# A two-layer decoder trunk on one core: the moving columns of every split product run from the last to the first

## What is computed

```
zxbcdt = rms(x) @ in_proj                  # 2048 x 10304
h = x + rms(gated_scan(zxbcdt) @ out_proj) # 4096 x 2048
h = h + rms(relu(rms(h) @ w1)**2 @ w2)     # 2048 x 8192, 8192 x 2048
k, v = rms(h) @ w_k, rms(h) @ w_v          # 2048 x 2048 each
h = h + rms(diff_attn(rms(h) @ w_q, k, v) @ o_proj)
h = h + rms(relu(rms(h) @ w1)**2 @ w2)
```

## Time and profile before

| what | value |
|---|---|
| median of three runs | 2656.3 us |
| span of the profiled execution, first to last instruction | 2654.2 us |
| granted TensorE clock, mean over the span | 0.988 of full |
| TensorE streams (PE) busy | 2578.9 us, 97% |
| weight loads (PEld) busy | 2338.9 us, 88% |
| VectorE (DVE) busy | 1805.5 us, 68% |
| ScalarE (ACT) busy | 1203.1 us, 45% |
| HBM read | 470.70 MB, 179 GB/s over the span |

### The profile page before, as it was taken

The page is one execution under the profiler, slowest core; times in us unless marked ns, Lnnn a source line. Parts: engine busy times, 40 slices in busy tenths (PEclk is TensorE's granted clock), DMA queues, the critical chain, the costliest instruction groups (busy, mean ns, idle before and its releaser), DMA issues.

```text
span 2654.2 us, 44813 instructions
## 1 busy us (share of the span) xinstructions
PE 2578.9 (97%) x16616; PEld 2338.9 (88%) x16616; DVE 1805.5 (68%) x2617; ACT 1203.1 (45%) x1589; POOL 138.4 (5%) x261
## 2 busy tenths in 40 slices
PE   6999999999999999999999899999899999999997
PEld 6889988998889898989898888988689999999996
DVE  3777777776876656565656867767876666666666
ACT  3555445544554434343434644444453434343433
POOL 2220222012100000000000000000000000000000
PEclk8999999999999999999999999999999999999999
DMA  8665566556446666566666555555356665666664
GB/s 182 199 189 176 172 192 196 166 181 190 160 141 193 190 190 190 190 190 189 190 189 191 175 167 166 158 175 167 120 169 196 185 194 186 193 186 194 187 193 135
DMA packets 267175, 477.17 MB, mean 180 GB/s; under 512 B 16577, under 2 KB 50210, under 8 KB 265298
## 3 DMA queue, kind: packets, MB, share of 16 engines
q1 hardware_dynamic: 263296, 457.76, 55.7%
q0 software_dynamic: 3296, 18.12, 2.8%
q10 hardware_dynamic: 498, 0.18, 0.0%
HBM read 470.70 MB, written 5.31 MB: 179 GB/s over the span
## 4 chain that ended last, share of the span: by engine, by line
PE 92%; DVE 4%; ACT 2%; issue 1%; DMA 1%; POOL 0%; ACTq 0%; DVEq 0%; POOLq 0%; SPq 0%
PE ps L1241 29%; PE ps L1242 29%; PE ps L1243 29%; PE ps L1387 1%; ACT whl L562 1%; DVE whl L820 1%; ACT junk L565 1%; PE ps L1406 0%; DVE h L929 0%; DVE xhl L890 0%; DMA par_rows<-a_conv_b 0%; PE ps L1466 0%; DVE stat L842 0%; PE ps L1380 0%; PE ps L1390 0%
## 5 line engine op out<-in xcount | busy, mean ns | idle before, releaser
L820 DVE TENSOR_TENSOR whl<-raw,whl 128x1024 fp32r<-128x1024 f32 x865 | 1069.8, 1237 | 771.3 <-ACT whl L562 761.9
L562 ACT ACTIVATE whl<-raw 128x1024 fp32r<-128x1024 f32 x865 | 916.2, 1059 | 1280.6 <-PE ps L1243 1253.9
L1241 PE MATMUL ps<-xhl,whl 128*128 128x256 f32 x3072 | 866.0, 282 | 6.3 <-DVE xhl L890 6.3
L1242 PE MATMUL ps<-xhl,whl 128*128 128x256 f32 x3072 | 859.2, 280 | 0.0
L1243 PE MATMUL ps<-xhl,whl 128*128 128x256 f32 x3072 | 858.7, 280 | 0.0
L1241 PEld LDWEIGHTS ps<-xhl,whl 128*128 128x128 f32 x3072 | 580.1, 189 | 11.4 <-DVE xhl L890 7.7
L1242 PEld LDWEIGHTS ps<-xhl,whl 128*128 128x128 f32 x3072 | 580.2, 189 | 2.9 <-issue 1.7
L1243 PEld LDWEIGHTS ps<-xhl,whl 128*128 128x128 f32 x3072 | 580.0, 189 | 0.0
L1241 PE MATMUL ps<-whl,bhl 128*128 128x512 f32 x1408 | 552.0, 392 | 4.7 <-DVE bhl L951 3.6
L1242 PE MATMUL ps<-whl,bhl 128*128 128x512 f32 x1408 | 550.5, 391 | 0.0
L1243 PE MATMUL ps<-whl,bhl 128*128 128x512 f32 x1408 | 549.9, 391 | 0.0
(11 more groups left out here) (194 smaller groups left out, 1877.6 us busy)
## 6 DMA issues: line engine op xcount, KB each, us to landing
raw<-mlp_w SPq DMA_DIRECT2D x512, 512.0 KB, 4.1
raw<-a_in_proj SPq DMA_DIRECT2D x161, 512.0 KB, 4.5
raw<-a_out_proj SPq DMA_DIRECT2D x64, 512.0 KB, 4.5
raw<-b_w_q SPq DMA_DIRECT2D x32, 512.0 KB, 3.7
raw<-w_k SPq DMA_DIRECT2D x32, 512.0 KB, 3.7
raw<-w_v SPq DMA_DIRECT2D x32, 512.0 KB, 3.7
raw<-b_out_proj SPq DMA_DIRECT2D x32, 512.0 KB, 3.7
cumb<-cum_scratch POOLq DMA_DIRECT2D x8, 1024.0 KB, 7.7
```

The source lines that it names most:

```text
L562: sc.activation(whi[:, s.split, :], raw[:, s.raw, :], ACT.Copy).then_inc(hi_ready, 1)
L820: ve.tensor_tensor(out=wlo[:, s.split, :], in0=raw[:, s.raw, :], in1=whi[:, s.split, :].bitcast(F32), op=ALU.subtract).then_inc(lo_ready, 1)
L1241: te.matmul(outs, lh, rh, start=start, stop=False, skip_group_check=True)
L1242: te.matmul(outs, lh, rl, start=False, stop=False, skip_group_check=True)
```

## The change

The helper `three` turns the moving operand and the output around: both are passed with a step of -1 along the columns. Column n of the moving operand still goes to column n of PSUM, so the values in PSUM are the same; the last column is read, multiplied and written first. The stationary operand, the flags, the order of the products, the waits and the number of instructions are as before.

```diff
             def three(outs, lhs, rhs, start, stop):

-                (lh, ll), (rh, rl) = lhs, rhs
+                (lh, ll), (rh, rl) = lhs, [t[:, ::-1] for t in rhs]
+                outs = outs[:, ::-1]
                 te.matmul(outs, lh, rh, start=start, stop=False, skip_group_check=True)
                 te.matmul(outs, lh, rl, start=False, stop=False, skip_group_check=True)
                 return te.matmul(outs, ll, rh, start=False, stop=stop, skip_group_check=True)
```

## The result

The changed kernel takes 2692.29 us (median of 4 runs, 2690.71 to 2694.12) against 2655.78 us for the kernel before (4 runs, 2653.08 to 2656.63). The ratio is 1.0137, with a 95% interval of 1.0125 to 1.0149: 36.5 us slower. The forecast was no change, 2656 us. The time lies in the stated range, where the rival "the remainder grows" had put 2687 us, but the likeliest case was the wrong one.

A forecast was written before the change was run, and what follows sets the result against it. TensorE was taken to bound the kernel, its products summing to 2403 us of a 2654.2 us span. Column price and remainder each added 0; with 2.1 us from span to run median, the forecast was 2656 us, range 2628 to 2740 us.

The forecast's parts named there:

- the remainder grows: Rival on TensorE: descending stream falls in step with the next stationary operand's load; 31 us more, 2687 us; chance 0.28.
- the likeliest case: Whole kernel: nothing changes, 2656 us, alone from 2650 to 2662 us; chance 0.37, the ineffective form included.
- What bounds the kernel: TensorE, streaming 97% of the span; time follows product distances one to one; loads, ScalarE and VectorE are hidden.
- The terms of the sum: TensorE's products: counts times distances, 1075 + 92 + 958 + 179 + 88 + 11 = 2403 us, 91% of the span.
- the five kinds: TensorE products: 256 columns moving `xhl` or `khl`; 512 columns against stationary `bhl`, `xhl` or `khl`; distances 116.7 to 233 ns.
- 190 us of remainders: Part of the 2403 us of TensorE products left beside 2212 us of columns at one per cycle.
- The price of a column: Moving read and PSUM write on TensorE: taken as unchanged, 0 us; upper bound 2379 us more.
- the rival at 4868 to 5035 us: TensorE: descending read or PSUM write takes two cycles a column; chance 0.18 for this or worse.
- The remainder: TensorE distance beyond one cycle a column, set by placement: taken as unchanged, bounds 90 us more to 28 us less.
- by symmetry: Moving stream's start: reversed, each kind keeps as many words in its first line, so the remainder changes by nought.
- The bound of 6.7 ns for wide products: 512-column `bhl` products: at worst each gains 6.7 ns, the gap between the two wide kinds; 28 us for 4224.
- The chances: Whole kernel: nothing changes 0.37, remainder grows 0.28, remainder shrinks 0.17, two cycles a column or worse 0.18.

The follow-up runs named there:

- run 3: Kernel before with the change made only for the products of 512 columns: 2685.75 us, ratio 1.0112.
- run 2: Kernel before with only the PSUM output written from last column to first, moving operand read ascending: 2656.44 us, ratio 1.0001.
- run 6: Kernel before, moving operand read in ascending blocks of 16 words, the words inside each from last to first: 3005.61 us, ratio 1.1315.
- runs 12 and 15: Kernel before, moving read in 4-word groups: words turned inside each (12), 2655.7 us, 0.9999; groups from last to first, words ascending (15), 2692.16 us, 1.0137.
- runs 5 and 14: Kernel before, moving read: 16-word blocks from last to first, words ascending (5), 2711.29 us, 1.0207; 8-word groups ascending, words turned inside (14), 2697.64 us, 1.0164.
- Run 4: Kernel before, all streams ascending, with the phase of `whl` moved from 0 to 60 bytes: 2658.44 us, ratio 1.0011.
- Runs 9 and 10: Phases of `xhl` and `bhl` swapped: in the kernel before (9), 2706.65 us, 1.0190; in the changed kernel (10), 2696.61 us, 1.0153; both ratios to the kernel before.
- run 8: Kernel before, second and third product of each three cut to 64 stationary columns and output rows, moving read descending: 2691.14 us, ratio 1.0135.
- run 7: Kernel before, second and third product of each three cut to 64 stationary columns and output rows, moving read ascending: 2671.74 us, ratio 1.0059.

## Why the prediction was wrong

- *What bounds the kernel*: right. The time followed the distances of the products, 35.4 us of span for 37.6 us of distances, and no other engine came on the path.
- *The terms of the sum*: right where it matters. The counts and distances of the five kinds are what the loss was found in, and run 3 added up from them. Two slips changed nothing: 78 of the 96 products of 64 columns ran 213 ns apart, in a stretch with a granted clock of 0.50 (34 to 53 us), so that their term is 18.7 us and not 11; and the "190 us of remainders" hold the 11 us of these products, the five kinds have 180.
- *The price of a column, taken as nought*: right for this change, as no product came near two cycles a column; the rival at 4868 to 5035 us fell. The write's part was nought within the noise (run 2). A column's price does rise with another order of the read: run 6 is at 1.25 cycles a column. PSUM — Partial Sum Buffer, Specifications, in the Trainium skill, has every non-contiguous pattern slow matmuls significantly; a descending run over adjacent words doesn't (1.0001). SBUF — State Buffer, in the Trainium skill, in the section on its two sides, has an access within the same 16-byte line at full bandwidth; runs 12 and 15 agree, where the order inside 16 bytes made no difference. But the rule says nothing of the order of the lines, and runs 5 and 14 keep at least two accesses on each line and lose some 6.6 ns a wide product: taken as a full condition for the rate, it isn't enough.
- *The remainder, taken as nought*: this step failed. I argued by symmetry that a stream keeps as many words in its first line when it starts from the top. Run 4 shows that the first word wasn't the question: a wide ascending stream with the descending one's start within 64 bytes costs 1.3 ns, not 6.6. I had read from the profile that the ascending remainders differ by placement, and so that 24 and 32 cycles are good cases of it; I should have asked what is left of a good case when the order in which it was got is turned round, and not whether its first word is alike. Runs 9 and 10 give the answer: 226.7 and 116.7 ns belong to ascending reads at these placements; descending reads cost 233.3 ns at both, and 117.8 and 118.3 ns. The term that I put at nought measured 16 cycles for a wide `bhl` product and not quite 3 for a narrow one of `xhl`. The change gave the placement's gain up.
- *The rival "the remainder grows"*, 2687 us with 0.28: right in its sign, and close by luck. It had 31 us in the narrow products and none in the wide ones; they took 10 and 27. Its mechanism, the stream in step with the next stationary operand's load, is not borne out: the loads stayed at 189 ns, and halving their columns left the descending wide stream where it was (run 8) and disturbed the ascending one (run 7). It isn't excluded either, as a clash that doesn't hang on the load's length would look the same. The bound of 6.7 ns for wide products, from `xhl` against `bhl` as stationary operand, was exact.
- *The chances*: I wrote that a change of start is likelier to leave the best case than to find a better one, and gave growth less than no change all the same. With three remainders out of five above the least, the rows bore growth as the likeliest case.

What stays open is the mechanism. The runs bound it: it is in the read of the moving operand; for wide products it sets in between 7 downward steps over blocks of 64 words and 31 over blocks of 16 (number of steps and length of block change together, so which of them counts isn't known), and doesn't grow after that; and it isn't in the words within 16 bytes. Why walking down over short blocks costs 16 cycles a wide product, and whether the 32 cycles of the ascending one hide the first few steps back, was not told apart. A stream with no load at all beside it wasn't tried.

## What to carry to other kernels

Where a kernel is bound by TensorE at full clock, split the distance of two products into columns and remainder: here 24 to 48 cycles of each are remainder, 180 us in all. Placement acted on it alone, and so did the downward reads, with one read order (run 6) that made the columns dearer. A difference between kinds of the same shape is a sign that a good case is in use, and a change of order can lose it. The worst kind seen is a bound for that and not a forecast: here it gives 28 us for the wide products, which took 26.7, and 31 us for the narrow ones, which took 9.9. Not every order loses it: in this kernel the direction of the PSUM write, the order of the words within 16 bytes and a few steps back over blocks of 64 words or more cost nothing.

## What the runs showed of the hardware that was not expected

- A descending read of the moving operand (fp32r) costs 233.3 ns for 512 columns, at both placements tried, and 117.8 or 118.3 ns for 256; an ascending one costs 226.7 or 233.3 and 116.7 or 120.0 ns, by placement.
- Turning the words in groups of 16 costs 40 ns per 512 columns, far more than reading all 512 downwards, and makes the distance 1.25 cycles a column for both widths; groups of 8 cost some 6.5 ns, groups of 4 nothing.
- Loading half as many stationary columns in two of three products, with half the output rows, made the kernel slower by 0.6%: the wide ascending distances scattered from 224 to 236 ns in place of a steady 226.7, and the narrow products took 14.3 us more.
